# Attention and recurrence of layer 0 cut into steps and placed between the quarters of the dense projections

## The reference

```python
mod = silu(c) @ ada_w[layer] + ada_b[layer]          # shift, scale, gate of each sequence
h   = rms_norm(x, norm_w) * (1 + scale) + shift
# layer 0
q_a, k_a, v_a, z_a, q_b, f_b, i_b, z_b = split(h @ w_in)
o_a = window_attention(rms(q_a), rms(k_a), v_a, cache, sinks)      # 16 heads, window 128
f   = lb + (1 - lb) * sigmoid(f_b);  k_b = (1 - lb) * sigmoid(-f_b)
S_t = f_t * S_(t-1) + k_t v_t^T;     o_b = rms_norm(q_t S_t)       # 8 heads, in chunks of 64
x   = x + gate * (concat(o_a * silu(z_a), o_b * silu(z_b)) @ w_out)
# layer 1
u, g_in, g_out, z = split(h @ w_in)
x   = x + gate * ((g_out * conv3(g_in * u) * silu(z)) @ w_out)
```

## Time and profile before

| | us |
|---|---|
| median of 3 runs | 1490.04 |
| lowest and highest | 1487.55, 1493.29 |
| profiled execution: time | 1484.24 |
| profiled execution: span, first to last instruction | 1482.5 |
| PE busy | 1410.3 (95%) |
| DVE busy | 748.0 (50%) |
| ACT busy | 572.0 (39%) |
| mean granted TensorE clock | 0.939 |

### The profile page before, as it was taken

One profiled execution on the slowest core, in us unless ns is written; L12 is line 12 of the kernel. 1 busy time (PEld: TensorE's weight loads), 2 busy tenths in 40 slices (PEclk: granted clock), 3 DMA queues, 4 the chain that ended last, 5 costly groups with the idle time before them and its releaser, 6 DMA issues.

```text
span 1482.5 us, 26698 instructions
## 1 busy us (share of the span) xinstructions
PE 1410.3 (95%) x10442; PEld 1280.6 (86%) x10442; DVE 748.0 (50%) x1494; ACT 572.0 (39%) x889; POOL 80.2 (5%) x161
## 2 busy tenths in 40 slices
PE   6899999999999898899999979999999999999997
PEld 3688889999999866666689969999999999999996
DVE  2445565335433477898544475345444453454442
ACT  4533334433332364444423254433434434333331
POOL 4000000000000021121100000000000000000011
PEclk9899999999999977666799989999999999999999
DMA  8999859788878810221377825564664555644551
GB/s 270 337 305 318 253 186 300 230 260 266 266 231 259 268 49 22 69 76 47 97 256 257 265 80 176 171 207 125 206 198 150 187 181 168 202 131 153 163 166 41
DMA packets 264155, 281.42 MB, mean 190 GB/s; under 512 B 9690, under 2 KB 260035, under 8 KB 263443
## 3 DMA queue, kind: packets, MB, share of 16 engines
q1 hardware_dynamic: 258332, 258.81, 54.8%
q0 software_dynamic: 5744, 21.51, 4.5%
HBM read 269.66 MB, written 12.47 MB: 190 GB/s over the span
## 4 chain that ended last, share of the span: by engine, by line
PE 84%; DVE 7%; issue 3%; DMA 3%; ACT 2%; SPq 0%; POOL 0%; ACTq 0%; POOLq 0%; DVEq 0%
PE pproj L576 21%; PE pproj L578 20%; PE pproj L577 20%; PE bank L586 4%; PE pproj L620 2%; PE pproj L622 2%; PE pproj L621 2%; PE bank L598 2%; DMA adaw<-in_ada_w 1%; PE bank L854 1%; PE bank L631 1%; PE pproj L879 1%; DMA acts<-xspill 1%; PE bank L658 1%; DMA acts<-in_x_sample 1%
## 5 line engine op out<-in xcount | busy, mean ns | idle before, releaser
L576 PE MATMUL pproj<-hh,wh 128*128 128x320 f32 x1856 | 580.7, 313 | 9.6 <-DVE hl L1455 6.5
L578 PE MATMUL pproj<-hh,wl 128*128 128x320 f32 x1856 | 576.3, 311 | 0.0
L577 PE MATMUL pproj<-hl,wh 128*128 128x320 f32 x1856 | 576.2, 310 | 0.0
L1357 DVE TENSOR_TENSOR wl<-raw,wh 128x1024 fp32r<-128x1024 f32 x260 | 317.3, 1224 | 442.9 <-ACT wh L1016 439.2
L1016 ACT ACTIVATE wh<-raw 128x1024 fp32r<-128x1024 f32 x260 | 274.7, 1058 | 504.4 <-PE pproj L578 322.8
L576 PEld LDWEIGHTS pproj<-hh,wh 128*128 128x128 f32 x1856 | 351.2, 189 | 23.9 <-issue 23.9
L577 PEld LDWEIGHTS pproj<-hl,wh 128*128 128x128 f32 x1856 | 351.4, 189 | 0.2 <-issue 0.2
L578 PEld LDWEIGHTS pproj<-hh,wl 128*128 128x128 f32 x1856 | 351.0, 189 | 0.0
L620 PE MATMUL pproj<-hh,wh 128*128 128x320 f32 x256 | 83.1, 325 | 2.7 <-DVE hl L1455 2.6
L576 PE MATMUL pproj<-yh,wh 128*128 128x320 f32 x256 | 79.7, 311 | 0.0
L621 PE MATMUL pproj<-hl,wh 128*128 128x320 f32 x256 | 79.5, 311 | 0.0
(11 more groups left out here) (347 smaller groups left out, 1444.4 us busy)
## 6 DMA issues: line engine op xcount, KB each, us to landing
adaw<-in_ada_w SPq DMA_DIRECT2D x192, 512.0 KB, 7.0
raw<-in_odd_w_in SPq DMA_DIRECT2D x128, 512.0 KB, 3.8
raw<-in_even_w_in SPq DMA_DIRECT2D x104, 512.0 KB, 8.9
raw<-in_even_w_out SPq DMA_DIRECT2D x32, 512.0 KB, 5.3
raw<-in_odd_w_out SPq DMA_DIRECT2D x32, 512.0 KB, 3.4
s<-in_state_hgrn POOLq DMA_DIRECT2D x8, 512.0 KB, 4.7
out_sh_s<-s POOLq DMA_DIRECT2D x8, 512.0 KB, 3.8
xspill<-acts POOLq DMA_DIRECT2D x1, 2560.0 KB, 11.2
```

The costliest lines, as they stand in the source:

```text
L576: mm(out, wh[:, q, k, cs], oph[:, kk, :], start=(kk == 0), stop=False)
L577: mm(out, wh[:, q, k, cs], opl[:, kk, :], start=False, stop=False)
L578: last = mm(out, wl[:, q, k, cs], oph[:, kk, :], start=False, stop=(kk == KC - 1))
L1357: tt(wl[:, q], raw[:, q], wh[:, q].bitcast(F32), ALU.subtract).then_inc(lo_ready, 1)
```

## The change

- The 18 units of `phases` and the first two of `out0` become one list `MID` of 80 quarters (n = 32 to 111). The units come in another order: i0, then qb, f, i three times, then za, zb. The first qb and the first f are now early units. The two units of `out0` in the list are mixed: their first halves come before their second halves.
- On PE, ACT and DVE a function `side(n)` issues the pieces of attention and recurrence after (on DVE before) the quarter or split of step n: one attention job per quarter from n = 36 (samples first), each in four stages over following quarters; one recurrence head per five quarters from n = 58 to 102. The roots are spread at n = 103 to 105.
- The attention outputs are written over the queries and later multiplied by the gates (`gate_z`), where before the gates were computed first.
- The double buffers of the recurrence are given up (`hbuf`, `qeb`, `vn`, `stt` one each, `s0` two instead of three), and the places of most small buffers in SBUF and PSUM are new. The jobs now share `bank[1]` to `bank[3]`.
- `ada_accumulate` gets a second wait, for `mod_done`, since the select of `MID`'s groups now writes into `bank[0]`. The function is used in `MID`, `out0` and `in1`. In `MID` `mod_out` comes at the third quarter of the unit; in `out0` and `in1` it stays where it was.
- `out0` keeps three iterations (six units), each unit with a group.
- `xspill` is written earlier, when all of h is ready; the caches are loaded at the 18th quarter and behind `xspill`; the residual is read back once the last head's outputs are done.

The core of the diff: `side` is PE's; the three loops over N0 to N1 are PE's, ACT's and DVE's in this order, and the last lines are POOL's.

```diff
+MID = [(U, q) for U in range(U_MID, U_OUT0) for q in range(4)] + [
+    (U_OUT0 + u, q) for u, q in ((0, 0), (0, 1), (1, 0), (1, 1), (0, 2), (0, 3), (1, 2), (1, 3))]
+N0, N1 = NE, NE + len(MID)
+UNITS = [("i", 0)] + [(x, n) for n in (1, 2, 3) for x in ("qb", "f", "i")] + [("za", n) for n in range(4)] + [
+    ("zb", n) for n in range(4)]
+J0, H0 = 36, 59
+    def head_step(n):
+        return divmod(n - (H0 - 1), 5)
...
         def ada_accumulate(G):
             pe.wait_ge(ada_out, G)
+            pe.wait_ge(mod_done, G)
             for s in range(4):
...
+        def side(n):
+            if n in (26, 28, 30, 32, 34):
+                head_sums((n - 26) // 2)
+            if 28 <= n < 31:
+                kv_rows(n - 28)
+            if 31 <= n < 35:
+                cached_keys(n - 31)
+            if 0 <= n - J0 - 3 < NJOB:
+                outputs(n - J0 - 3)
+            if 0 <= n - J0 - 2 < NJOB:
+                probs_t(n - J0 - 2)
+            if 0 <= n - J0 < NJOB:
+                scores(n - J0)
+            h, r = head_step(n)
+            if r == 0 and 1 <= h <= HH:
+                head_outputs(h - 1)
+            if r == 0 and 0 <= h < HH:
+                v_rows(h)
+            if r == 1 and 0 <= h < HH:
+                hgrn_scores(h)
+            if r == 1 and 1 <= h <= HH:
+                square_sum(h - 1)
+            if r == 2 and 0 <= h < HH:
+                k_rows(h)
+            if r == 3 and 0 <= h < HH:
+                prompt_updates(h)
+                sample_scores(h)
+                from_sample_states(h)
+            if r == 4 and 0 <= h < HH:
+                sample_updates(h)
...
+        for n in range(N0, N1):
+            U, q = MID[n - N0]
+            if U < U_OUT0 and q == 0:
+                ada_accumulate(U + 8)
+            mid_quarter(n)
+            if U < U_OUT0 and q == 1:
+                ada_select(U + 8, bank[0][:, UC:UC + 2 * NSEQ])
+            side(n)
         def out0(i):
             for p in range(2):
-                extra = not (isinstance(i, int) and 2 * i + p in (0, 7))
...
+                ada_accumulate(32 + 2 * i + p)
+                unit((i + U_OUT0 // 2, i * 2 + U_OUT0 + p), p, hh, hl, KC)
+                ada_select(32 + 2 * i + p)
+        with pe.Fori(1, 4) as i:
             out0(i)
...
+        for n in range(N0, N1):
+            split_early(n + 3)
+            if n == N0 + 1:
+                forget_gates(0)
+            U = (n - N0) // 4 + U_MID - 1
+            if n % 4 == 0 and U_MID <= U < U_OUT0:
+                evacuate(U)
+            if n % 4 == 0 and U + 1 < U_OUT0:
+                ada_evac(U + 9)
+            side(n)
...
+        for n in range(N0, N1):
+            if n == N0:
+                add_partial(NE - 1)
+            side(n)
+            split_early(n + 3)
+            U = (n - N0) // 4 + U_MID - 1
+            if n % 4 == 0 and U_ZA <= U < U_OUT0:
+                gate_z(U - U_ZA)
+            if n % 4 == 2 and U + 1 < U_OUT0:
+                mod_out(U + 9, bank[0][:, UC:UC + 2 * NSEQ])
...
         def out0(i):
             for p in range(2):
                 def evac():
                     residual(i, p, 32, xc_new, acts[:, ds(C_X1 + 4 * i + 2 * p, 2), :])
...
+                    add_squares(2 * i + p)
                 around(U_OUT0 + 2 * i + p, evac)
-                if not (isinstance(i, int) and 2 * i + p in (0, 7)):
-                    mod_out(33 + 2 * i + p)
+                mod_out(32 + 2 * i + p)
...
+        pool.wait_ge(quarter_used, 18)
+        pool.dma_start(ckn[:], a["cache_k"][0].rearrange("b s k d -> s b (k d)")).then_inc(k_in, 16)
         pool.wait_ge(xc_act, KC)
-        pool.wait_ge(quarter_used, NE)
+        pool.wait_ge(h_ready, KC)
         pool.dma_start(xspill, acts[:, C_X0:C_X0 + KC, :].rearrange("p c t -> p (c t)")).then_inc(stored, 16)
```

More of the change, by code:

```diff
@@ new lines, in square_sum, with k_rows @@
+        def square_sum(h):
+            pe.wait_ge(g_osq, h + 1)
+            pe.wait_ge(g_x, h + 1)
+            mm(bank[3][:, 0:T], ones[:], osq[:], start=True, stop=True).then_inc(g_sum, 1)
+        def k_rows(h):
+            if h == 0:
+                pe.wait_ge(j_g, NJOB)
+            else:
+                pe.wait_ge(g_ms, h)
+            ke = hbuf[:, O_KD:HB]
+            for t in range(3):
+                r = P if t < 2 else NS
+                last = tr(bank[3][0:r, t * P:t * P + P], ke[:, t * P:t * P + r], ident[:])
+            last.then_inc(g_kt, 1)
@@ new lines, in head_outputs @@
+        def head_outputs(h):
+            pe.wait_ge(g_st, h + 1)
+            pe.wait_ge(g_s, 4 * h + 4)
+            pe.wait_ge(g_onsb, h + 1)
+            for c in range(4):
+                rows, t = slice(64 * (c % 2), 64 * (c % 2) + 64), c // 2
+                out = bank[2][:, 64 * c:64 * c + 64]
+                if c:
+                    mm(out, sst[:, c - 1, :], qeb[:, 64 * c:64 * c + 64], start=True, stop=False)
+                    pe.wait_ge(g_o, 6 * h + c)
+                mm(out, vn[rows, t, :], s_t[rows, t, :], start=(c == 0), stop=True).then_inc(g_o, 1)
+            pe.wait_ge(g_o, 6 * h + 4)
+            mm(bank[2][:, SEQ:T], vn[0:NS, 2, :], s_t[0:NS, 2, :], start=True, stop=False).then_inc(g_o, 1)
+            pe.wait_ge(g_o, 6 * h + 5)
+            for e in range(2):
+                last = mm(bank[2][:, SEQ + 32 * e:SEQ + 32 * e + 32], onat[:, e, :], place[:], start=False, stop=(e == 1))
+            last.then_inc(g_o, 1)
@@ L869, in prompt_updates @@
-        def prompt_updates(h):
-            vn = vns[:, h % 2]
-            pe.wait_ge(g_ksb, h + 1)
-            if h >= 1:
-                pe.wait_ge(g_s, 4 * h)
-            for half in range(2):
-                rows = slice(64 * half, 64 * half + 64)
-                for t in range(2):
-                    c = 2 * t + half
-                    last = mm(pproj[:, 0, c * P:c * P + P], ken[rows, t, :], vn[rows, t, :], start=True, stop=True)
-                last.then_inc(g_u, 1)
-                pe.wait_ge(g_u, 3 * h + half + 1)
@@ L1294, in _ @@
+        with act.Fori(1, 4) as i:
             out0(i)
-        out0(3)
         token_rsqrt(1)
```

1411 lines of the change are left out of this document (729 added, 682 removed).

## The result

The changed kernel takes 1569.57 us (median of four runs, 1567.0 to 1574.67), the kernel before 1488.8 beside it. The ratio is 1.0544, with a 95% interval of 1.0505 to 1.0583. The forecast was 1500 with a range of 1474 to 1540: the sign was right, the size wrong by 70 us, and the time lies outside the range. Some executions take over 1.5% longer than the fastest of the same kernel (none of these, three of four in experiment 3, one of ten in experiment 5), and ratios with an interval leave them out.

What follows compares the result with a forecast made beforehand. PE was taken to bound the dense stages, with a slow stretch to fill: 1484.2 - 88.5 + 12.5 + 60.6 + 20 + 6 = 1494.8 us, plus 5.8 to the median, 1500.6, stated as 1500; range 1474 to 1540.

Steps and rivals of the forecast that it cites:

- The content of the middle: Stretch from `phases`' end to `out0`'s last matmul: units, groups, attention and recurrence need 267.4 us without PE waits, saving 88.5.
- The added wait: PE stops for `mod_done` before 5 groups in `out0` (4.76 us each) and 7 in `in1` (5.25 each): +60.6 us.
- Rival three: In the loops `mod_done` runs ahead, so the new wait is met in time: 1420 us, chance 0.07.
- The clock behind the stops: In `out0` and `in1`, the clock falls behind 85% of the 12 stops, 2.0 us each: +20 us, between 0 and 34.
- Waits in the middle: In the middle, PE's waits for DVE and ACT cost 5 us, as both engines' work fits within PE's time.
- Switches: In the middle, each of some 70 pieces adds a switch of 0.11 us: 7.5 us.
- The clock in the middle: A fall after 3 in 10 of 12 pieces with little streaming, 1.7 us each: +6 us, between 0 and 25.
- The price worked out for it, 1614 us: Rival in which the clock swings at every piece in the middle, 70 falls at 1.7 us: 1614 us, chance 0.04.
- POOL's new order: Earlier cache loads and x store, at about quarters 18 and 24, cost nothing, as key rows come some 18 us later.
- Rival one: TensorE keeps full clock through the 5 us stops and the middle's pieces: 1475 us, chance 0.17.
- rival two: Engines run in lockstep in the middle, 1 us lost at each of 45 recurrence steps: 1540 us, chance 0.22.
- The signs: In the timeline after: `in1` groups 5 us late by `mod_out`; middle 28 + 297 + 141 + some 20 us, clock near 1.00.

Runs made afterwards that it cites:

- experiment 3: Changed kernel, but in the middle SP issues each unit's ada weights behind its projection weights, not ahead; 1532.0 us median, 1508.6 us in the profiled execution.
- experiment 5: Kernel before, its ada loads rewritten in the 18 units from 210 to 509 us, but the same transfers issued in the same order; 1488.0 us, 0.9976 of before.
- experiment 2: Kernel before, with only PE's wait for `mod_done` added at the head of each `in1` iteration; 1538.4 us, +50.4 against 1488.0.
- experiment 1: Changed kernel, with PE's wait for `mod_done` kept only in the middle and left out in `out0` and `in1`; 1486.8 us, 0.9994 of before.
- experiment 6: Changed kernel with both edits: `mod_done` wait only in the middle, ada weights loaded behind projection weights; run twice, 1437.9 and 1429.6 us.
- experiment 4: Changed kernel, but in the middle ACT does its pieces before `split_early`, loads issued as they were; 1536.8 us, 1.0339 of before.

## Why the prediction was wrong, point by point

**The content of the middle, 267.4 us with all eight units and six groups, -88.5: right.** Without the waits the middle takes 477.6 us (experiment 3), where the forecast's own terms give 28 + 297 + 141 = 466, and 484.5 with its switches, waits and clock.

**The added wait, +60.6: right.** The row reads 63.8 us. In `out0` the stops are 5.73, 4.91, 4.96, 4.90 and 4.93 us, 25.4 together for 23.8, and in `in1` 5.42 to 5.47 for 5.25. All 12 stops came. Rival three, the wait met in time, fell with this.

**The clock behind the stops, +20: right, slightly small.** `out0` takes 134.8 us for 98.8 of content and 25.4 of waits, which leaves 10.6 for five stops, 2.1 each. Experiment 2 gives 1.9. All 12 were followed by a fall (each group behind one takes 3.3 to 3.6 us for 1.93) and not 85% of them, so 24. Together experiment 1 gave back 82.8 us where the forecast had 80.6. The right sign of the forecast rests on this wait and its clock alone.

**Waits in the middle, 5 of the +12.5: the step that failed.** It says "PE's piece of step n needs what DVE and ACT did in the same step" and then adds up only durations of ACT's and DVE's instructions, 16 and 21.5 us against 31. The forecast never asks when the weights arrive that ACT's first instruction in the step waits for. The change put the pieces behind `split_early` on ACT, and SP's order puts 2 MB in front of the quarter that this split needs. Neither shows in a sum of busy times. PE was idle for 35.8 us in the middle, not 5, and for 3.6 with the loads in the other order. With the clock, that order cost 49 to 57 us (experiment 6 against 1). Experiments 3 and 4 show it from two sides. "Of a step that is queued behind another, ask what the other one waits for" was missing, and the old kernel's trace could have told it: ACT had only 104.6 us of work in the 296 us of the earlier trace rows, and what it did with most of the rest was to wait for weights (158.5 us, the row in experiment 5). I read that as spare time for pieces.

**Switches, 7.5 of it: not separated.** With the clock at 1.00 for most of the middle, the profile of experiment 3 leaves 11.6 us above 466 for switches, waits and the rest of the clock together.

**The clock in the middle, +6: mis-sized.** It was 28 us in the profiled execution, 501.6 less the 474.0 of busy time in experiment 3. The mechanism stood in the forecast ("the risk is the pieces with little streaming: a head's outputs"), but it expected a fall after 3 in 10 of them, at 1.7 us. In the profile with both edits six heads' outputs were followed by one, at 2.8 us, in another four, at 1.6, in experiment 3 none; and in the changed kernel the idle times of the waits probably add falls of their own.
The rule that the forecast weighed, the Trainium skill, "TensorE: Matmul & The Clock Gate", section "A second HAM failure mode: psum-queue depth-cycling", bears on it: short idles between groups of matmuls make the clock swing. The traces agree in part. The clock does swing, but at the blocks of small products and behind the stops, not at each of some 70 pieces, and in the kernel with both edits in stretches of 5 us in which PE is idle for 0.1 us at most. The price worked out for it, 1614 us, was not reached.

**POOL's new order, at nothing: half wrong.** The first group comes 13.5 us later (223.2 for 209.7). From 165 us on PE has 7.8 us more of busy time (48.1 for 40.3). Of these, 4.3 are the transposes of key rows and cached keys that the forecast had in its 141, and most of the rest goes with the clock, 0.91 for 1.00. And it has 5.7 us more of idle time, in which PE waits for ACT: 5.4 us for the scale of the head norms, where it was 2.2, and 2.6 for the copies of key and value rows. Some 6 us of the place are no more than the spread of executions: the first group starts at 209.7 to 215.05 us in the three profiles in which the old kernel is unchanged up to there, and at 222.8 to 228.6 in the eight of the changed kernel and its variants. Neither the cache copies nor the early x store showed an effect. Why ACT is late there is open: the coupling of head norms and key rows with ACT wasn't tried.

**The rivals.** The nearest was two, 1540 us, "a piece on PE waits for DVE or ACT". It was right in what is seen and wrong in why: it put it down to splits that wait for PE's last quarter, and to engines near their limit. It would have given 1540, and the clock of the middle as measured, 28 us for 6, another 22, still short of 1569.6. Rival one (the clock holds) fell: all 12 stops were followed by a fall. A rival that takes transfers and queues together, "weights late in front of the pieces", was missing, and the range ended at 1540 for want of it.

**The signs.** The forecast named the right ones: the middle should take some 486 us, and "if that stretch is longer by tens of us, rival two holds, and the waits on PE name who was late". It was 537, and the waits named ACT. From there it took one more step back, from ACT's idle time to the transfer and to SP's queue.

## What to carry to other kernels

Before putting latency-critical pieces into an engine's in-order stream, look at what that stream already waits for, and how far ahead: waits for transfers, 158.5 us in 18 units, were free in front of splits alone, and one of 8.4 us became 9 us of PE's time when a piece that PE needed stood behind it. Big transfers that are needed late belong behind the small ones that are needed soon, in the issuing queue. And a wait added in a shared helper is paid in every loop that calls it; here 83 us went to loops in which the banks didn't need it.

## What the runs showed of the hardware

TensorE's clock can fall while PE counts as busy: late in a block of small dependent products (outputs of 64 and 32 columns) it went to 0.50, its lower level of 1.2 GHz, and stayed there for up to 5 us of dense matmuls (experiment 6), with PE idle for 0.1 us at most. Whether it falls there differs from execution to execution (none, four and six times in three profiles whose middle is the same), so one profile isn't enough to price it. With triplets of dense matmuls between the products it did not fall once in 232 us, but with the blocks whole it did not in the 225 us of experiment 3 either.

Behind stops it fell every time: 19 stops of 4.9 to 5.7 us (12 in the changed kernel, 7 in experiment 2), at some 2 us beyond each stop.
